# Low parts of the queries held once and multiplied with 64 rows, and a ring of four query tiles instead of three

## What is computed

```
def fox_attend(q, k, v, cq, ck, q_pos, k_pos):
    s = jnp.einsum('bqhd,bkhd->bhqk', q, k).astype(jnp.float32) * (HEAD_DIM ** -0.5)
    s = s + (jnp.transpose(cq, (0, 2, 1))[..., :, None] - jnp.transpose(ck, (0, 2, 1))[..., None, :])
    mask = k_pos[None, :] <= q_pos[:, None]
    s = jnp.where(mask, s, jnp.finfo(jnp.float32).min)
    p = jax.nn.softmax(s, axis=-1).astype(v.dtype)
    return jnp.einsum('bhqk,bkhd->bqhd', p, v)
```

## Time and profile before

| | |
|---|---|
| Median of 3 runs | 2550.39 us (2548.34 to 2554.64) |
| The profiled execution | 2548.34 us, span 2546.5 us |
| Stage of prompt attention and pages | about 1686 to 2395 us of the span |
| TensorE busy over the span | 90% (15044 matmuls) |
| GpSimd busy over the span | 45% |
| HBM, read and written | 403.58 MB and 60.65 MB |

### The profile page before, as it was taken

How to read it: one execution, slowest core, us unless ns; L and a number is a source line. 1 busy time by engine, 2 the same in 40 slices (tenths; PEclk the granted TensorE clock), 3 DMA queues, 4 the chain that set the end, 5 groups by cost and what they waited for, 6 DMA issues and landing times.

```text
span 2546.5 us, 44564 instructions
## 1 busy us (share of the span) xinstructions
PE 2284.5 (90%) x15044; PEld 1844.7 (72%) x15044; DVE 1390.6 (55%) x1990; ACT 949.7 (37%) x1622; POOL 1145.8 (45%) x802
## 2 busy tenths in 40 slices
PE   5999999997449998979999899877999999999799
PEld 4999999997249998969888686634454545545399
DVE  4789988899791016566785211023545455454523
ACT  4556655655351013223332121323343443434311
POOL 0798889988563214444445332232232232222211
PEclk7999999999669998989999999988999999999999
DMA  3222222222033121135635788899999999997312
GB/s 110 73 73 67 72 80 64 73 74 70 18 114 123 45 89 53 65 126 163 182 138 182 258 280 295 287 361 365 387 347 349 349 360 363 357 360 277 117 48 81
DMA packets 143702, 464.36 MB, mean 182 GB/s; under 512 B 28001, under 2 KB 36578, under 8 KB 142386
## 3 DMA queue, kind: packets, MB, share of 16 engines
q1 hardware_dynamic: 117954, 384.07, 43.2%
q0 software_dynamic: 22848, 62.56, 7.4%
q10 hardware_dynamic: 2736, 15.60, 1.5%
HBM read 403.58 MB, written 60.65 MB: 182 GB/s over the span
## 4 chain that ended last, share of the span: by engine, by line
PE 53%; POOL 12%; DVE 11%; issue 8%; DMA 8%; ACT 5%; SPq 2%; ACTq 0%; POOLq 0%; DVEq 0%
POOL ACC L1385 7%; PE PS L610 5%; PE PS L608 5%; PE PS L609 5%; PE PS L703 4%; PE PS L826 4%; PE PS L769 4%; PE PS L705 4%; PE PS L704 4%; PE PS L910 4%; DMA KV<-ck 3%; DMA KV<-cv 3%; PE PS L921 2%; PE PS L895 2%; PE PS L616 2%
## 5 line engine op out<-in xcount | busy, mean ns | idle before, releaser
L1358 POOL TENSOR_TENSOR WL<-RAW,WH 128x1024 fp32r<-128x1024 f32 (+1 forms) x113 | 283.6, 2510 | 454.4 <-ACT WH L995 447.9
L1710 DVE SCALAR_TENSOR_TENSOR PS<-UX,CWT,PS 128x1024 f32<-128x1024 f32 (+1 forms) x672 | 466.3, 784 | 0.0
L641 PE MATMUL PS<-HH,WH 128*128 128x384 f32 (+1 forms) x1152 | 378.9, 329 | 20.7 <-DVE HL L1696 20.7
L643 PE MATMUL PS<-HH,WL 128*128 128x384 f32 (+1 forms) x1152 | 377.8, 328 | 0.0
L642 PE MATMUL PS<-HL,WH 128*128 128x384 f32 (+1 forms) x1152 | 377.6, 328 | 0.0
L703 PE MATMUL PS<-GH,WH 128*128 128x384 f32 (+1 forms) x792 | 272.4, 344 | 29.8 <-DVE KC L1820 16.2
L1385 POOL TENSOR_TENSOR ACC<-ACC,PROD 128x1088 f32<-128x1088 f32 x112 | 284.7, 2542 | 31.3 <-ACT PROD L1047 25.1
L705 PE MATMUL PS<-GH,WL 128*128 128x384 f32 (+1 forms) x792 | 263.5, 333 | 0.0
L704 PE MATMUL PS<-GL,WH 128*128 128x384 f32 (+1 forms) x792 | 262.6, 332 | 0.0
L641 PEld LDWEIGHTS PS<-HH,WH 128*128 128x128 f32 x1152 | 217.6, 189 | 24.7 <-issue 13.7
L1602 POOL DMA_DIRECT2D QI<-qX_scr x128 | 77.7, 607 | 326.4 <-PE PS L879 324.9
(11 more groups left out here) (224 smaller groups left out, 4667.8 us busy)
## 6 DMA issues: line engine op xcount, KB each, us to landing
KV<-ck SPq DMA_DIRECT2D x256, 512.0 KB, 6.7
KV<-cv SPq DMA_DIRECT2D x256, 512.0 KB, 6.4
RAW<-wA SPq DMA_DIRECT2D x48, 512.0 KB, 3.6
RAW<-wP SPq DMA_DIRECT2D x16, 640.0 KB, 3.8
zT_scr<-ZS ACTq DMA_DIRECT2D x16, 544.0 KB, 2.7
Z<-zT_scr SPq DMA_DIRECT2D x16, 544.0 KB, 3.6
RAW<-wB SPq DMA_DIRECT2D x17, 512.0 KB, 3.7
RAW<-wO SPq DMA_DIRECT2D x16, 512.0 KB, 3.6
```

The source lines that it names most:

```text
L641: pe.matmul(out, WH[w][:, kk], HH[:, k, a:b], start=k == 0, stop=False)
L643: mm = pe.matmul(out, WL[w][:, kk], HH[:, k, a:b], start=False, stop=k == KD - 1)
L1358: pool.tensor_tensor(WL[s][:, 0:n], RAW[s][:, 0:n], WH[s][:, 0:n].bitcast(F32), ALU.subtract).then_inc(s_lo, 1)
L1710: i = dve.scalar_tensor_tensor(out=o, in0=x, scalar=w[:, j:j + 1], in1=o, op0=ALU.mult, op1=ALU.add)
```

## The change

Tile `QI` has three planes instead of four: both heads' low parts share one plane, head 0 in partitions 0 to 63 and head 1 in 64 to 127. L879 takes only the 64 partitions of its head, from the query tile and from the key tile. The zeros are gone, and with them six memsets on GpSimd (L1629) and the wait for them. A tile is filled by three DMAs instead of four; the bytes are the same. The freed space makes a fourth tile, and the loads are placed anew: blocks 0 to 3 of the next pair are loaded at t = 10, 12, 14 and 15 of the pair before it, blocks 4 to 7 at t = 2, 4, 6 and 8.

```
-        QI = [m(f"QI{s}", [P, 4, P], F32R) for s in range(3)]
+        QI = [m(f"QI{s}", [P, 3, P], F32R) for s in range(4)]
...
-                    pe.wait_ge(s_qi[q % 3], 64 * (q // 3 + 1))
+                    pe.wait_ge(s_qi[t // 2 % 4], 96 * b + 48 * (t // 8 + 1))
...
-                    mm = pe.matmul(out[:, 0:e - a], queries[:, 2 + hl, :], KX[par][:, hl, a:e], start=False, stop=True)
+                    mm = pe.matmul(out[:, 0:e - a], queries[HD * hl:HD * hl + HD, 2, :],
+                                   KX[par][HD * hl:HD * hl + HD, hl, a:e], start=False, stop=True)
...
-            def load_queries(q):
+            def load_queries(b, i):
...
                 for half in range(2):
-                    pool.dma_start(dst[rows, 2 + half, :].bitcast(F32), qX[b, 1, rows, cols]).then_inc(s_qi[q % 3], 16)
+                pool.dma_start(dst[:, 2, :].bitcast(F32), qX[b, 1, :, cols]).then_inc(s_qi[i % 4], 16)
...
-            for s in range(3):
-                for half in range(2):
-                    pool.memset(QI[s][HD - HD * half:P - HD * half, 2 + half, :].bitcast(F32), 0.0).then_inc(s_pad2, 1)
-            pool.wait_ge(s_pad2, 11)
...
-                if x > 0 and t % 2 == 0 and x // 2 + 2 < NQ * PAIRS:
+                if t in (2, 4, 6, 8):
                     pool.wait_ge(s_s, x)
-                    load_queries(x // 2 + 2)
+                    load_queries(b, 4 + t // 2 - 1)
...
+                if t in (10, 12, 14) and not last:
+                    pool.wait_ge(s_s, x)
+                    load_queries(b + 1, t // 2 - 5)
+                if t == 15 and not last:
+                    pool.wait_ge(s_s, x + 1)
+                    load_queries(b + 1, 3)
```

More of the change, by code:

```diff
@@ L275, in build @@
         s_q, s_wo = [sem(f"keys_in{s}") for s in range(2)], [sem(f"wo_in{s}") for s in range(2)]
-        s_qi = [sem(f"queries_in{s}") for s in range(3)]
+        s_qi = [sem(f"queries_in{s}") for s in range(4)]
         s_knh, s_knl, s_kx = sem("normed_hi"), sem("normed_lo"), sem("parts_out")
@@ L862, in scores @@
                 n = P * (item + 1)
-                q = 8 * b + t // 2
-                queries = QI[q % 3]
+                queries = QI[t // 2 % 4]
                 if t == 0:
@@ L1592, in _ @@
             store_g(PAIRS - 1)
-            def load_queries(q):
-                b, i = q // NQ, q % NQ
+            def load_queries(b, i):
                 cols = slice(P * order[i], P * order[i] + P)
-                dst = QI[q % 3]
+                dst = QI[i % 4]
                 for half in range(2):
-                    rows = slice(HD * half, HD * half + HD)
-                    pool.dma_start(dst[rows, 0:2, :].bitcast(F32),
-                                   qX[b, 0, :, cols].rearrange("(h d) n -> d h n", d=HD)).then_inc(s_qi[q % 3], 16)
-                    pool.dma_start(dst[rows, 2 + half, :].bitcast(F32), qX[b, 1, rows, cols]).then_inc(s_qi[q % 3], 16)
+                    pool.dma_start(dst[HD * half:HD * half + HD, 0:2, :].bitcast(F32),
+                                   qX[b, 0, :, cols].rearrange("(h d) n -> d h n", d=HD)).then_inc(s_qi[i % 4], 16)
+                pool.dma_start(dst[:, 2, :].bitcast(F32), qX[b, 1, :, cols]).then_inc(s_qi[i % 4], 16)
             def load_v(b):
@@ L1626, in _ @@
             pool.wait_ge(s_unit, U_TAIL - U_OUT)
-            for s in range(3):
-                for half in range(2):
-                    pool.memset(QI[s][HD - HD * half:P - HD * half, 2 + half, :].bitcast(F32), 0.0).then_inc(s_pad2, 1)
-            pool.wait_ge(s_pad2, 11)
-            load_queries(0)
+            load_queries(0, 0)
             pool.wait_ge(s_vst, 32 * PAIRS)
             load_v(0)
-            load_queries(1)
+            load_queries(0, 1)
             for s in range(2):
@@ L1637, in _ @@
             load_z(0)
-            load_queries(2)
+            load_queries(0, 2)
+            load_queries(0, 3)
             for x in range(N_SLOTS):
```

## The result

The changed kernel takes 2581.85 us in the median of 4 runs (2581.56 to 2583.72); the kernel before, measured beside it, 2552.51 us. The ratio is 1.0127, with a 95% interval from 1.0111 to 1.0141: it is slower, by 29 us by the medians and 32 us by the ratio. Forecast were slower, 2586 us, and a range from 2547 to 2610. The profiled execution took 2586.07 us, span 2584.2 us.

A forecast was written before the change was run, and what follows sets the result against it. Pages were taken to bound the first pair, TensorE the other seven. Added TensorE work of 57.5 us, less 7, 5, 5 and 3 us of cover, gave 37.5 us over 2548.3: 2586 predicted, range 2547 to 2610.

The forecast's parts named there:

- The first rival: At L879: a change of rows is free, leaving 0 to 3 us of gain from the queries, 2545 to 2550; 12%.
- Into the shape: Before each of 192 L879 matmuls: 0.10 us for the shape change plus 0.10 for the bare load, 38.4 us.
- Out of it: From L879 to L873, L766 or L895: 0.14 us each, 14.6 us for 104 places and 4.5 for 32.
- My further 0.04: At exits from L879: 0.04 us for the next matmul's bare bf16 weight load, on top of 0.10 for the shape change.
- Before L826: At the 42 places where L826 follows L879: a change of shape stands there already, so they cost nothing.
- The signs: In the profile after: L873 to L879 about 0.2 us longer, L879 to L873 near 0.35, pairs 1 to 7 some 5 longer.
- What took it back: Cover for TensorE's added 57.5 us: first pair 7, page waits 5, output-add waits 5, queries 3 us.
- I had 13 for the first three: Pairs 1 to 7: cover from page waits 5 us, output-add waits 5, query-tile waits at most 3.
- I had all covered: First pair, bound by pages: its eighth of the added TensorE time, 7 us, covered by them.
- The 3 us: TensorE's waits for query tiles, 0.9 us at the matmul and 2.2 at the weight load: at most 3 us gained.
- The third rival: Query loads were the wait: up to 69 us could go, a quarter taken, 2531, only where row changes are free; 5%.
- The pages as the bound: Rival: the page stream sets the pace, so TensorE's 57 us of added work hide under it, 2548 to 2555; 5%.

The follow-up runs named there:

- experiments 1 and 3: experiment 1, and the changed kernel with a long block's two 64-row matmuls side by side after the step's others: 2567.95 us, ratio 1.0041 to the kernel before.
- experiment 4: Kernel before with 64-row low-part matmuls in the first pair only: 2557.55 us, ratio 1.0003; in another kernel, for head 0 only: 2567.6 us, ratio 1.005.
- experiment 1: Kernel before with only the low-part matmul cut to its head's 64 partitions, old ring and four loads kept: 2588.91 us, ratio 1.0119.
- experiment 2: Changed kernel, ring of four and new loads, but the low-part matmul over all 128 partitions of the shared plane: 2545.53 us, ratio 0.9957.

## Why the prediction was right

**The mechanism.** TensorE bounds pairs 1 to 7, and a change of rows from 128 to 64 is a change of shape: shown by experiments 1 and 3 and by the two forms in one trace in experiment 4. The one kind of place that had it already, before L834, had told it right. The rule of the drain (the Trainium skill, "TensorEngine Tiling (Array Packing)", Key Properties) agrees: 0.09 us of it at each change here. The first rival, a free change of rows, is out.

**The terms.** Into the shape I had 0.10 + 0.10 for 192, that is 38.4 us; measured are 0.09 + 0.10, 36.5 us. Out of it, before bias, page scores and transposes, I had 0.14; measured is 0.09. The distance there grows by 0.19, but 0.10 of that is the entry's bare load, counted already. My further 0.04 for the next load doesn't show before bias and page scores, which load bf16; before the transposes, which load fp32, it is 0.05 us, 2 us in all. For 136 exits the 0.09 is 12.2 us and not 19.1. Before L826 the change of shape costs nothing more, as predicted. Together that is 48.7 us on TensorE, where I had 57.5; the 2 us before the transposes and what the 32 places with 128 columns save cancel.

**The signs.** The sum was right and the places were not. I put the bare load ahead of the matmul: L873 to L879 0.2 us longer, L879 to the next L873 0.35 us, L879 to L826 unchanged. Measured are 0.09 us longer, 0.43 us, and 0.43 instead of 0.33. The load stands in the distance behind the matmul. The other signs came: the tile as 64*128, the load starting with its matmul, pairs 1 to 7 longer by 4.3 us each, a DMA share below 1 there, no wait for `QI`. One reading was wrong without harm: in the last two slices of the stage the DMA engines stand at 7 and 3 tenths, not at 9.

**What took it back.** Of the 48.7 us some 30 came through by the times, about 19 were covered, where I had 20. How the cover divides is less sure. In pairs 1 to 7, with 42.6 us of the work, the first two profiles differ by 30.1 us, and the lists of waits account for most of the other 12.5: pages 4.8, output add 9.6 less 6.0, query tiles 2.2, ScalarE's 2.1 less 0.8, in sum 11.9 us. I had 13 for the first three. In the first pair, with 6.1 us, I had all covered; the time of experiment 4 says that 0.8 us came through, the profiles say more. And the profile of the kernel before was of its fastest run, so that the two profiles differ by 37.7 us in their whole spans, while the times differ by 29 to 32. The sum ended there and not at 37.5 because the work added to TensorE was put 9 us too high, not because of the cover. By the medians the miss is 4 us.

**The queries.** Here a term was mis-sized: the ring is worth 9 to 11 us with 128-row matmuls, not 3. The 3 us were read from the profile of the fastest run, which had few of these waits, and left out what the clock loses behind one. It didn't spoil the sum, which was luck: in the changed kernel no gain of the ring can be seen. With the old ring (experiment 1) the loss is 1.19%, with the new one 1.27%, a difference of -2 us, give or take 5. The trace of experiment 1 shows no wait for a query tile in pairs 1 to 7. When TensorE is slower the tiles are in time anyway. The third rival named this gain and asked for free row changes as its condition; with 128-row matmuls, which change no rows (experiment 2), the time was 2545.5 us, between my 3 us and its 2531.

**The pages as the bound.** Out for pairs 1 to 7. In the first pair they cover some of the added work; how much stays open (experiment 4).

## What to carry to other kernels

Before cutting the rows of a matmul to half, look at what stands before and after it: alone among 128-row neighbours it streams no faster and costs two changes of shape and a bare weight load, 0.28 us here. Placed together, on both halves of the array and in different banks, the same 64-row matmuls only broke even with the 128-row ones on the same ring; they paid (0.3%) when the bias joined them, so that eight streams shared one entry. When a change has two parts, compare with the kernel that has only the other part: against the kernel before, the ring's gain would have passed for one of the half rows. And an earlier load is worth only what the slower engine hasn't already given: measure it in the version that you mean to keep.

## What the hardware showed that was not expected

- The two row halves ran side by side without any setting for it: 2 x 384 columns in 0.38 us with entry and exit, where one alone, in the changed kernel, took 0.37.
- Behind a change of shape, a bare bf16 weight load of 128 columns doesn't show in the distances; a bare fp32 one cost 0.10 us at the 64-row matmul and 0.05 us at the first transpose after it.
- A wait of some 2.5 us in a full stretch can cost more than itself: in three profiles the granted clock fell to 0.50 right behind one.
- The fastest of several runs is a poor witness for waits: the first profile's span of the kernel before was 2546.5 us, a later one's 2559.3, with twice the wait for query tiles (2.2 and 4.4 us).
